# Windowed attention by bands of 32 queries and 160 keys, with block transposes on VectorE

## What is computed

```python
q, k, v, z = jnp.split(x @ w_in, ...)     # 16 query heads, 2 key/value heads, head size 64
q, k = _rope(q, pos), _rope(k, pos)
# blocks of W = 128 queries; keys of the block before and of the own block
s = jnp.einsum("bnqhgd,bnkhd->bnhgqk", qb, kb) * HD ** -0.5
rel = qi + W - kj
valid = (rel >= 0) & (rel < W) & (blk * W + kj - W >= 0)
s = jnp.where(valid, s, -jnp.inf)
p = softmax(concatenate([s, sink], -1))[..., :-1]   # a learned sink for each head
o = jnp.einsum("bnhgqk,bnkhd->bqnhgd", p, vb)
return (o * silu(z)) @ w_out
x = layernorm(alpha * x + y)
```

## Time and profile before

| | before |
|---|---|
| median of 3 runs | 1020.15 us |
| profiled execution | 1020.63 us |
| its span | 1018.9 us |
| PE busy | 993.9 us (98%) |
| DVE busy | 675.4 us (66%) |
| ACT busy | 462.2 us (45%) |
| POOL busy | 291.7 us (29%) |
| granted clock of TensorE, mean | 0.998 |

### The profile page before, as it was taken

How to read it: one execution, slowest core, us unless ns; L and a number is a source line. 1 busy time by engine, 2 the same in 40 slices (tenths; PEclk the granted TensorE clock), 3 DMA queues, 4 the chain that set the end, 5 groups by cost and what they waited for, 6 DMA issues and landing times.

```text
span 1018.9 us, 17445 instructions
## 1 busy us (share of the span) xinstructions
PE 993.9 (98%) x6318; PEld 813.1 (80%) x6318; DVE 675.4 (66%) x1296; ACT 462.2 (45%) x1349; POOL 291.7 (29%) x647
## 2 busy tenths in 40 slices
PE   7999999999999999999999999999999999999997
PEld 6888787888788787888888888888787777776885
DVE  4677768586867676754456766533447888788655
ACT  4655466575756666644355111302126545556000
POOL 1008483828474746563000000000102222221000
PEclk9999999999999999999999999999999999999999
DMA  6232414133241324234113212302000010014211
GB/s 211 64 104 68 119 42 110 52 67 96 42 120 37 114 47 106 55 87 115 42 41 144 85 42 65 102 11 73 1 21 22 22 43 21 23 63 115 93 42 62
DMA packets 89974, 71.04 MB, mean 70 GB/s; under 512 B 32768, under 2 KB 79008, under 8 KB 89888
## 3 DMA queue, kind: packets, MB, share of 16 engines
q1 hardware_dynamic: 55568, 53.07, 17.4%
q10 hardware_dynamic: 34320, 16.84, 6.6%
HBM read 59.38 MB, written 10.52 MB: 69 GB/s over the span
## 4 chain that ended last, share of the span: by engine, by line
PE 82%; DVE 7%; ACT 6%; DMA 3%; issue 2%; ACTq 0%; DVEq 0%
PE ps L741 28%; PE ps L928 14%; PE ps L1000 9%; PE ps L1105 8%; PE ps L1130 3%; PE ps L941 2%; PE ps L1089 2%; DVE tok L1524 2%; PE ps L1117 2%; PE ps L898 1%; PE ps L909 1%; DMA ws_raw<-in_b_w_in 1%; PE ps L907 1%; PE ps L818 1%; PE ps L886 1%
## 5 line engine op out<-in xcount | busy, mean ns | idle before, releaser
L741 PE MATMUL ps<-act_hi,w_hi 128*128 128x512 f32 x512 | 223.6, 437 | 0.2 <-DVE w_lo L1475 0.2
L741 PE MATMUL ps<-act_hi,w_lo 128*128 128x512 f32 x512 | 201.1, 393 | 0.0
L741 PE MATMUL ps<-act_lo,w_hi 128*128 128x512 f32 x512 | 200.2, 391 | 0.0
L1524 DVE SCALAR_TENSOR_TENSOR tok<-xs,convw,tok 128x512 f32<-128x512 f32 x144 | 115.9, 805 | 15.5 <-ACT xs L1236 13.7
L672 POOL TENSOR_TENSOR rank<-inverse,tok 128x60 f32<-128x60 f32 (+24 forms) x248 | 98.2, 396 | 96.2 <-DMA tok<-blocks_in 78.0
L741 PEld LDWEIGHTS ps<-act_hi,w_lo 128*128 128x128 f32 x512 | 96.1, 188 | 21.2
L741 PEld LDWEIGHTS ps<-act_hi,w_hi 128*128 128x128 f32 x512 | 97.0, 189 | 12.2 <-issue 0.4
L741 PEld LDWEIGHTS ps<-act_lo,w_hi 128*128 128x128 f32 x512 | 97.2, 190 | 10.0
L675 POOL TENSOR_TENSOR inverse<-inverse,rank 128x60 f32<-128x60 f32 (+24 forms) x248 | 97.5, 393 | 19.4
L928 PE MATMUL ps<-wo_hi,act_hi 128*128 128x512 f32 x224 | 88.4, 395 | 1.0 <-DVE wo_lo L1627 1.0
L928 PE MATMUL ps<-wo_lo,act_hi 128*128 128x512 f32 x224 | 87.5, 391 | 0.0
(11 more groups left out here) (273 smaller groups left out, 2187.0 us busy)
## 6 DMA issues: line engine op xcount, KB each, us to landing
w_raw<-in_a_w_in ACTq DMA_DIRECT2D x32, 512.0 KB, 4.3
tok<-in_x SPq DMA_DIRECT2D x8, 512.0 KB, 7.1
decay<-gc_rows SPq DMA_DIRECT2D x8, 512.0 KB, 5.5
tok<-blocks_in SPq DMA_DIRECT2D x32, 128.0 KB, 2.6
v_turn<-v_tok SPq DMA_DIRECT2D x8, 512.0 KB, 6.0
v_tok<-v_turn SPq DMA_DIRECT2D x32, 128.0 KB, 2.9
xres<-in_x SPq DMA_DIRECT2D x8, 512.0 KB, 3.6
ws_raw<-in_b_w_in SPq DMA_DIRECT2D x16, 256.0 KB, 2.7
```

Of the source, the lines that this page charges most:

```text
L741: mm = pe.matmul(ps[:, g % 2, :], lhs[:, k, :], rhs[:, k, HALF * b:HALF * (b + 1)], start=(i == 0), stop=(i == GROUP - 1))
L1524: ins = dve.scalar_tensor_tensor(conv[b], xs[:, b, k:k + HALF], convw[:, k, tile:tile + 1], conv[b], ALU.mult, ALU.add)
```

## The change

Each unit's 128 queries are four bands of 32. A band's 32 queries see 159 keys, which lie in 160 consecutive ones (five blocks of 32), from the block that holds the first query's oldest key to the band's own.

- `logits`: for each head and band a product of 32 queries by 160 keys, on tiles of 64 x 32: 16 matmuls for a unit, on eight tiles of the array. The scale 1/8 is put on the queries as they are copied to bT.
- `biased`: only the first and the last block of 32 keys need a mask, added from `edges`. The sink lies as a 161st column beside the keys, so that the maximum and the exponentials cover it; the maximum is written negated.
- Normalizing goes from DVE to POOL, `low_gate` too. The merging copy, the PE transposes, `probs` and the `affine_select`s go.
- `turned`: DVE turns the probabilities in blocks of 32 x 32 (in a band, a key's row then is its number in its block of 32).
- `values`: for that, the values of every block of 32 keys must lie at each band's 32 partitions. ACT's copy of the values (`vv`) is written to device memory by SP, and read back four times, as `v_rows`, one copy for each group of 32 partitions. `v_rows` takes the place of projection weights, so it can't be read before the projections end; SP's reads stand between the wait for z_los 2 and the load of `z_raw` for j = 2. Then a unit is 5 blocks x 4 bands x 2 pairs of heads = 40 matmuls of 32 rows by 64 columns of weights and 64 columns of data, on eight tiles. Each band has a bank of its own: three in banks 5 to 7, the fourth in a bank of the logits.
- `branch` takes three bands on DVE, one turn later than before, `last_rows` the fourth on ACT.

The core of the diff:

```diff
+def unit(v):
+    k = v // 2
+    x = (k + v) % 2
+    return k, x, k // 4, 2 * (k % 4) + x
+def last_rows_bank(k):
+    return 4 if k == PAIRS - 1 else 1 + 2 * ((k + 1) % 2)
...
-            sp.wait_ge(q_group, NT)
+            sp.wait_ge(q_val, NT)
+            sp.dma_start(v_rows_out.rearrange("t p d -> p t d"), vv[:, :, :]).then_inc(s_vd, 16)
             for j in range(NK):
                 if j:
                     sp.wait_ge(z_los, j)
+                if j == 2:
+                    sp.wait_ge(s_vd, 16)
+                    sp.wait_ge(q_group, 3 * NT)
+                    for a in range(4):
+                        sp.dma_start(v_rows[32 * a:32 * a + 32, :, :],
+                                     v_rows_out.rearrange("t (b i) d -> i (t b) d", b=4)).then_inc(s_vr, 16)
                 sp.dma_start(z_raw[:, :, :], ...)
...
+            for v in range(UNITS):                       # POOL
+                k, x, jj, n = unit(v)
+                probs = logit[k % 2][x][:, :, 0:WIDE]
+                pool.wait_ge(s_rden, v + 1)
+                pool.tensor_tensor(probs, probs, sm["rden"][:, k % 2, x, :].unsqueeze(2).broadcast_to([P, 4, WIDE]),
+                                   ALU.mult).then_inc(s_norm, 1)
+                if v % 4 == 0 and v // 4 + 1 < NK:
+                    low_gate(v // 4 + 1)
...
+            def logits(v):
+                k, x, jj, n = unit(v)
+                if k:
+                    pe.wait_ge(s_e, place(k - 1, x) + 1)
+                if k >= 2 and v % 2:
+                    pe.wait_ge(s_ob3, k - 1)
+                for b in range(2):
+                    for a in range(4):
+                        at = n * P + 32 * a
+                        for e in range(2):
+                            r = 64 * e
+                            mm = pe.matmul(ps[32 * a:32 * a + 32, 1 + 2 * x + e, 256 * b:256 * b + WIDE],
+                                           bT[r:r + 64, 2 * jj + b, at:at + 32], kd[r:r + 64, jj // 2, at:at + WIDE],
+                                           start=True, stop=True)
...
-                turn_probs(2 * k)
-                turn_probs(2 * k + 1)
...
+            def values(v):
+                k, x, jj, n = unit(v)
+                kv = jj // 2
+                pe.wait_ge(s_pt, v + 1)
+                if v == 0:
+                    pe.wait_ge(s_vr, 64)
+                if v % 2 == 0:
+                    pe.wait_ge(s_e, min(v + 3, UNITS))
+                    if k:
+                        pe.wait_ge(s_ob, 2 * k)
+                for i in range(BAND):
+                    for a in range(4):
+                        row = 4 * (n - 1) + a + i
+                        if row < 0:
+                            continue
+                        bank = last_rows_bank(k) if a == 3 else VALUE_BANK + a
+                        for e in range(2):
+                            mm = pe.matmul(ps[64 * e:64 * e + 64, bank, 64 * x:64 * x + 64],
+                                           v_rows[32 * a:32 * a + 32, row, 64 * kv:64 * kv + 64],
+                                           prob[32 * a:32 * a + 32, x, i, 2 * e:2 * e + 2, :].rearrange("p h q -> p (h q)"),
+                                           start=(i == 0 or row == 0), stop=(i == BAND - 1))
...
+            def turned(v):                               # DVE
+                k, x, jj, n = unit(v)
+                dve.wait_ge(s_norm, v + 1)
+                if k:
+                    dve.wait_ge(s_pv, 2 * k)
+                dve.transpose(prob[:, x].rearrange("p c h q -> p h c q"),
+                              logit[k % 2][x][:, :, 0:WIDE].rearrange("p h (c i) -> p h c i", i=32)).then_inc(s_pt, 1)
...
             for k in range(PAIRS - 1):                   # DVE
                 biased(2 * k + 2)
                 biased(2 * k + 3)
-                normalized(2 * k + 2)
-                if k % 2 == 0 and k // 2 + 1 < NK:
-                    low_gate(k // 2 + 1)
-                normalized(2 * k + 3)
+                if k:
+                    branch(k - 1)
+                turned(2 * k)
+                turned(2 * k + 1)
+                inverted(2 * k + 2)
                 if k >= 4 and k % 4 < 2:
                     apply_gate(k // 4 * 2 - 2 + k % 4)
+                inverted(2 * k + 3)
...
                 gate(k + 1)
-                branch(k)
+            turned(UNITS - 2)
+            turned(UNITS - 1)
+            branch(PAIRS - 2)
...
+            def last_rows(k):                            # ACT
+                jj, n = k // 4, 2 * (k % 4)
+                act.wait_ge(s_pv, 2 * k + 2)
+                act.activation(bT[...][:, :, :, 3, :], ps[:, last_rows_bank(k), 0:P]..., ACT.Copy, scale=0.5)\
+                   .then_inc(s_ob3, 1)
```

More of the change, by code:

```diff
@@ L55 @@
 TOKEN_BANKS = (0, 1, 6, 7)
-LOGIT_BANKS = (1, 3)
-GATE_BANK, VALUE_BANK, PROB_BANK = 0, 5, 6
-TURN_BANKS = [2 + n % 2 for n in range(3 * NT - 3)] + [VALUE_BANK, VALUE_BANK, PROB_BANK]
+BAND = 5
+WIDE = 32 * BAND
+GATE_BANK, VALUE_BANK = 0, 5
+TURN_BANKS = [2 + n % 2 for n in range(3 * NT - 3)] + [5, 5, 6]
 PAIRS = UNITS // 2
@@ L298, in hybrid_trunk @@
         zt = sbuf(stz, "zt", [P, HALF])
[L299 to L302, removed]
+        room0 = sbuf(stz, "room0", [P, 16])
+        v_rows = sbuf(stz, "v_rows", [P, 4 * NT, P])
+        prob = sbuf(stz, "prob", [P, 2, BAND, 4, 32])
+        logit = [[None, None], [None, None]]
+        logit[1][0] = sbuf(stz, "logit10", [P, 4, WIDE + 1])
+        sm = {n: sbuf(stz, "sm_" + n, [P, 2, 2, 4]) for n in ("neg", "sum", "rden")}
         room1 = sbuf(stz, "room1", [P, (raw_at - 512 - 12 * DM - taken[0]) // 4])
@@ L309, in hybrid_trunk @@
         z_hi[0] = sbuf(stz, "z_hi0", [P, NK, P], F32R)
-        room4 = sbuf(stz, "room4", [P, DM])
-        logit_far = sbuf(stz, "logit_far", [P, 2, 4, P])
-        logit = [(logit_far, logit_near)[u // 2][:, u % 2] for u in range(4)]
+        for side in range(2):
+            logit[0][side] = sbuf(stz, f"logit0{side}", [P, 4, WIDE + 1])
+        logit[1][1] = sbuf(stz, "logit11", [P, 4, WIDE + 1])
         stz.close()
@@ L690, in _ @@
             steps.next(pool.memset(kd[:, :, 0:P], 0.0))
[L691 to L692 removed]
+            steps.next(pool.memset(corner[:, :, :], 0.0))
             steps.wait()
[L695 removed]
+            steps.next(pool.affine_select(out=corner[:, 0, :], in_=corner[:, 0, :], compare_op=ALU.is_gt, fill=NEG,
+                                          base=0, pattern=[[1, P]], channel_multiplier=-1))
+            steps.next(pool.affine_select(out=corner[:, 1, :], in_=corner[:, 1, :], compare_op=ALU.is_ge, fill=NEG,
                                           base=0, pattern=[[-1, P]], channel_multiplier=1))
+            steps.next(pool.memset(first_band[:, :], 0.0))
+            steps.wait()
+            for a in range(4):
+                rows = slice(32 * a, 32 * a + 32)
+                steps.next(pool.tensor_copy(edges[rows, :, :], corner[rows, :, rows]))
+                steps.wait()
+                steps.next(pool.tensor_copy(first_band[rows, WIDE - 32:WIDE], corner[rows, 1, rows]))
+                steps.wait()
+                steps.next(pool.memset(first_band[rows, 0:P - 32 * a], NEG))
+                steps.wait()
             pool.wait_ge(z_his, 1)
@@ L701, in _, with low_gate @@
                 .then_inc(z_los, 1)
[L703 to L710, removed]
+            def low_gate(j):
+                pool.wait_ge(z_his, j + 1)
+                if j >= 2:
+                    pool.wait_ge(z_group, 2 * (j - 1))
+                pool.tensor_tensor(z_lo[j % 2][:, :, :], z_raw[:, :, :], z_hi[j % 2][:, :, :].bitcast(F32),
+                                   ALU.subtract).then_inc(z_los, 1)
+            for v in range(UNITS):
[6 more added lines that the diff above has]
+                    low_gate(v // 4 + 1)
         @block.tensor
@@ L1071, in _ @@
                 turn_tokens(n - 2)
[L1072 to L1091, removed]
+            pe.wait_ge(q_c, 17)
+            def logits(v):
[12 more added lines that the diff above has]
+                                           start=True, stop=True)
                 mm.then_inc(s_s, 1)
@@ L1297, in high_wo @@
                     act.wait_ge(s_group, 2 * TILES)
+                elif k == 1 and i == 1:
+                    act.wait_ge(z_t, PAIRS)
                 elif k == 2 and i == 1:
```

165 lines of the change are left out of this document (65 added, 100 removed).

## The result

The changed kernel takes 1028.79 us (median of 4 runs, 1027.4 to 1029.8); the kernel before took 1021.08 beside it (1019.94 to 1022.21). The ratio is 1.0075, with a 95% interval of 1.0054 to 1.0095: slower by 0.5 to 1%. Forecast were 1005 us and a range of 998 to 1016. The profiled execution has a span of 1026.2 us (1027.97 in all), 7.3 more than before; all that follows is read from it.

The account below looks back on a forecast made before the run. PE, busy 98% of the span, was taken as the bound. From 1020.63 us, +7.5 up to gate(2), -21.1 for 13 turns and -2.1 for the tail, in all -15.7, gave 1004.9, say 1005 us; 8-in-10 range 998 to 1016.

Parts of the forecast that it names:

- The hole: Before the first values: PE stands for 7 us waiting for the v_rows transfer, values(0) at 781.1 instead of 774.57.
- The clock: Behind the wait for v_rows: up to 6 us of PE work at half rate, loss 0 to 3, taken as 2.5 us.
- Values 1.17 us a pair: Each turn's values on PE: 20 rounds of 55 to 60 ns on eight tiles, 1.17 us a pair.
- rival 3: Values on PE: one record per 11 ns, 1.8 us a pair, +10 us, 1015 in all; chance 0.10.
- The logits: Each turn's logits on PE: 8 rounds of 135 ns on eight tiles, 1.1 us a pair.
- the changes of form: Between the pieces of a turn on PE: 0.1 to 0.25 us each, in all 0.45.
- The tail: From gate(15)'s start to out_pair(1,1): 12.6 us instead of 14.69, saving 2.1.
- rival 4: Attention stage: elementwise work becomes the bound, gate(m+1) 1.2 us late every second turn, +8, 1013 us; chance 0.10.
- rival 2: Values and logits: tiles sharing a row group do not overlap, a turn is 12.7 us, 1062 in all; chance 0.08.
- the rule named beside it: Values on PE: weight loads overlap running matmuls only in another row group, giving 7.6 us a pair.
- a gain of 21 us in the turns: From gate(2) to gate(15): 13 turns of 8.47 us instead of 10.09, saving 21.1 us.
- the point of no return: A turn's non-gate part: above 3.9 us the change becomes slower (13 x 0.42 and the tail's 2.1 equal the hole's 7.5).

Follow-up runs that it names:

- e8_late_mask_before: The kernel before, with its first causal select on POOL repeated 20 times ahead of the first unit: 1034.51 us, ratio 1.0116.
- e3: e1_early_rows with the values' products of the second pair of heads left out except in the last block of keys: 1001.28 us (one run).
- e4: e1_early_rows with the values' products taking 32 data columns instead of 64, except in the last block of keys: 1017.98 us (one run).
- e6_pair_at_once: e1_early_rows with one matmul taking all four heads, 80 records for a pair's values instead of 160: 1006.06 us, ratio 0.9843.
- e9_pair_mid_gate: e6_pair_at_once with the out_raw load held back until the last values, and values moved ahead of the gate matmuls' last third: 1028.65 us, ratio 1.007.
- e1_early_rows: The changed kernel with the v_rows reads issued right behind the z_raw load for j = 1: 1017.71 us, ratio 0.9969.
- e10_pair_at_once_late_rows: The changed kernel with only the widened products of e6_pair_at_once, the v_rows reads left where the change put them: 1015.84 us, ratio 0.995.

## Why the prediction was wrong

The forecast of 1004.9 us for the profiled execution was missed by 23.1. By its own steps:

- *The hole.* Right in place, cause and start of the copies (low_gate(1) ended at 770.93, forecast 770.9). Values(0) came at 783.34, not 781.1: the transfer was mis-sized, 205 GB/s instead of 263. I had taken the v_tok window for a proof that 32 partitions are no bound; its packets averaged 0.9 KB, these are 512 bytes at 43 ns.
- *The clock.* Forecast 2.5 us; the first values and logits took 4.49 us to gate(2) instead of 2.7, and the gate behind them 6.48 instead of 5.77, together 2.5. Right, and e8_late_mask_before shows the same price (about 2) by itself. With both, gate(2) is at 787.83 instead of 786.3: 1.5 us of the miss.
- *Values 1.17 us a pair: the step that failed first.* They took 1.89. The rows showed a record per 11 ns, and I set that aside because three tiles had been too few to show a shorter spacing. The trace has 10.9 ns, e3 and e4 show that it doesn't follow the columns. This is rival 3 (1.8 a pair, at a chance of 0.10). The logits, 1.25 to 1.31, were forecast at 1.1. Together with the changes of form these are about 3.2 us a turn instead of 2.7. A turn without stops is 8.95 us, not 8.47: 13 x 0.48 = 6 us of the miss.
- *The instruction supply: in no step and no rival.* The stops add 0.75 us to the mean turn, 13 x 0.75 = 10 us, the largest part. The page of the kernel before had the line of q8, 51 packets, and the number of PE's records; the density of the new loop, 448 records in 3 us, could have been set beside it. With 160 records fewer a turn (e6_pair_at_once) the stops of the stage are gone.
- *The tail.* To out_pair(1,1) 12.6 us forecast, 17.45 measured, and 0.6 more behind it at the clock of 0.50: 5.5 of the miss. Values(15) start 12.0 us behind gate(15) instead of 10.9 and take 5.5 us with their drain instead of 1.6; 3.2 of that is the stop, which belongs to the supply again.
- *The elementwise chain* (rival 4) didn't bound the stage in the changed kernel: PE's waits in it are "issue" but for 1.4 us ahead of gate(1). It did as soon as an edit closed a ring through it, in e9_pair_mid_gate. *Tiles that share a row group* (rival 2) overlap: a pair's 160 records, with their loads, went out in 1.74 us, where that rival had 2.2 and the rule named beside it 7.6. The rule that was weighed there (the Trainium skill, TensorE: Matmul & The Clock Gate, Part 3, The mechanism), that a load overlaps running matmuls only in another row group, isn't borne out by these rows.

Sum: 1.5 + 6 + 10 + 5.5 = 23. The sign turned because a gain of 21 us in the turns shrank to 5, which the hole of 9 us then outweighed, and the tail lost 2.8 us instead of gaining 2.1. Rival 2 had named the point of no return, a non-gate part above 3.9 us in a turn, and the measured mean is 9.70 - 5.77 = 3.93; but that point counted on the tail's 2.1, so that the two agree only by chance.

## What to carry to other kernels

Splitting a product into many small tiles doesn't only cost columns: count the records. Here a matmul with its load went out every 11 ns at best, and 256 of PE's instructions that pass before the next block is there end in a stop that no wait of the program explains (from the start of one block to the next it took 2.6 to 4.9 us at the changed kernel's stops). Where a pause stands in the middle of a group, number the instructions, the sequencer's too, before looking for a semaphore. Halving the number of products at twice the width was worth 12 us, as much as taking away a hole of 9 us. And ask of each move of work between in-order engines which ring it lengthens: one third of a gate's matmuls put behind the values instead of ahead of them cost 23 us.

## What was not expected of the hardware

- PE's instructions come, as read from the stops, in blocks of 256 (packets of 16.4 KB); every such stop, in six kernels, is at the same count modulo 256, and PE goes on 1.2 to 1.5 us after the packet lands. What happens between the landing and the restart isn't in the trace.
- The pace: 10.9 ns for a matmul record of 32 x 64 weights and 64 columns on eight tiles, 10.4 with mostly 32 columns.
- 512-byte packets from device memory into 32 partitions took 43 ns each, into 128 partitions 28. Whether it is the partitions or the four copies of the same rows was not tried.
- The runs of kernels with stops spread more: e1_early_rows 1014.61 to 1021.55, e6_pair_at_once 1005.87 to 1006.45. But e10_pair_at_once_late_rows, which has the hole, spread as far without them, and the kernel before ran from 1020.13 to 1025.01 beside e1_early_rows; the cause stays open.
